# Two norms in front of first panels: raw scaled residual multiplied chunk by chunk, token factor applied at the evacuation

## The chip, the cores and the metric

One Trainium2 chip, one core. The metric is the device time of one execution in microseconds (us). The kernel before was timed three times: 2372.38 us median, 2368.09 lowest, 2375.34 highest. One more execution was profiled; all rows below come from it.

## The reference, cut to what matters

Two transformer stages run one after the other on 256 tokens of width 1024. The first has two layers with feed-forward blocks and attention; its result passes through a norm (`norm_final`) and goes straight into the second stage, which begins with a norm of its own (`norm_mix_2`) and a projection `w_in_2` into four groups of columns. At its end the second stage adds `merged @ w_o`, norms again (`norm_ffn_2`, no shift) and multiplies with `ffn_w_up_2`, then a short convolution over the tokens, a gated product and a last down projection.

What matters here is that each of the two norms is `x * r(token) * gain(feature)`, where `r` is the inverse root of the token's mean square, and that a matrix product follows it. The token factor stands outside the sum over features, so `(x * r * gain) @ W` equals `r * ((x * gain) @ W)`.

## The kernel before, in words

**Layout.** The residual `h` is held as 8 chunks of 128 features (partitions) by tokens; in the part that matters only the 256 tokens of the first stream. Weights come from DRAM as panels: one panel is 16 tiles of 128x128 in the phases here, 1 MB, and gives two output chunks. `st.load` (L500 to L510) issues a panel's DMA on SP into one of two `raw` buffers, once the buffer's last reader is done.

**Three products.** Every float32 product is made from split operands: `hi` is a rounded copy, `lo` the rest. `three` (L1181) issues three matmuls for one tile: whi with u_hi, whi with u_lo, wlo with u_hi. A panel of these phases is 8 chunks by 2 outputs by 3, or 48 matmuls of 128x256. Splitting a panel costs ACT one copy (L566) and DVE one subtraction (L568). `split` (L558 to L569) is issued one panel ahead.

**Order.** All engines run queues in program order. `Stream.run` (L626 to L715) writes it: for each group the split of the next panel, the evacuation of the last group, then the product of this one; PE waits for its panel's `s_lo` (L672) and for the evacuation two groups back (L674). With `split_first` the split stands ahead of the evacuation. Panel 1 of a phase that follows a norm is not split by `split` but in four quarters, `split_hi` and `split_lo` (L599 to L624), placed between the steps of the norm. The last of them, quarter 3 of `lo`, raises `s_lo` for panel 1, and it is issued at the very end of `norm` (L1172).

**The norm.** Squares of the chunks are added into `ssq` as the chunks of `h` are finished (`add_square`, L980); the last chunk's square is kept apart (`last_squares`, L999). `norm_scale` (L1026) has PE add over the features with one-column products (L1037, L1040), ACT takes the root (L1052), DVE the inverse (L1055) and spreads it on a diagonal (L1056), and PE turns that into a row factor in a PSUM bank (L1064). `norm` (L1081) then makes `u_hi` and `u_lo` of all chunks: the first two one by one (L1110, L1126, L1136), then three pairs (L1118, L1145, L1148, L1153). At both places of the change the first panel's product goes chunk by chunk behind this (L1196 to L1200, and L1992 to L1995), so that each pair of chunks is multiplied as soon as it is there.

**First norm** (after `down2` of layer 1, ahead of `rwkv_in`): called with `twice`, it makes the factor of two norms in a row, bank 5, and the factor of the first, bank 4. After it come a memset, a small DVE operation for `rest_mu` (L1958), the scaling of `h` in place (`scaled_rows`, L1887, in four pairs), and the side panels. `side_panels` (L2048) issues panel n in four quarters and, after the first quarter of panel n, the evacuation of panel n-1 (`side_evac`, L2005) and then the split of panel n+1. For `rwkv_in` the evacuation is two ACT copies for each output, L2014 and L2015, and one DVE operation, L2022. Panel 2's first three quarters are followed on PE by the `w_a_g` products (L2122), which wait for a sigmoid and a tanh on ACT (L2117, L2118), and everything of the second stage follows these. While this norm runs, POOL builds `rel_bias_map`.

**Second norm** (after `w_o`, ahead of `up_2`): one factor. `w_o` has four groups and `split_first`; its evacuation `wo_evac` (L2855) adds two chunks to `h` and squares them. `up_evac` (L2892) copies a group's two outputs to `conv_in` and makes `conv_out` from the same banks on ACT, then the taps on DVE.

These few lines set the order in the norm:

```
        for x in parts:
            pe.after(*(squared if x == 1 and twice else [squared[x]]))
            act.after(pe.do(sums(x, tmp, False, True)))
...
        marks = [None, None]
        for x in parts:
            pe.after(scaled[x])
            marks[x] = pe.do(pe.q.matmul(banks[4 + x][:, 0:S], cst("ones"), diag[:, x * S:(x + 1) * S], start=True, stop=True))
...
        before[0](*before[1:])
        if ph:
            st.split_lo(ph, 1, 3)
```

Of the kernel before, what the change touches and what calls it, by code (L numbers as in the profile page):

```python
# [16 lines left out]
F32 = mybir.dt.float32  # L17
# [5 lines left out]
P = 128  # L23
D = 1024
KC = D // P
S = 256
# [691 lines left out]
def build(nc, ins, out):  # L718
# [32 lines left out]

    sil = [sb(f"sil{i}", [P, T]) for i in range(2)]
# [273 lines left out]
    def norm_scale(n, twice=False, then=None):  # L1026

        parts = (1, 0) if twice else range(n // S)  # L1030
        tmp, squared = last_square

        def sums(x, src, start, stop):

            for t in range(2):
                both = twice and x == 1
                m = pe.q.matmul(banks[4 + x][:, t:t + 1], src[:, x * S + t * P:x * S + (t + 1) * P], cst("ones", 1),  # L1037
                                start=start and t == 0, stop=stop and t == 1 and not both)
                if both:
                    m = pe.q.matmul(banks[5][:, t:t + 1], src[:, t * P:(t + 1) * P], cst("eps", 1),  # L1040
                                    start=False, stop=stop and t == 1)
# [213 lines left out]
    def down(name, n, gates, hidden, then, weight=None):  # L1255

        q0 = sq_count[0]
# [11 lines left out]
        def evacuate(m, par, G, done):  # L1269
# [9 lines left out]
        def square(m, par, G):  # L1279
# [5 lines left out]
            add_square(at(m), n, count=k, weighted=weighted)  # L1285

# [86 lines left out]
    for l in range(L1):  # L1373
# [500 lines left out]
        if last:  # L1874
            both_gains = sb("both_gains", [P, KC])
            dve.do(dve.q.tensor_tensor(both_gains[:, :], vcol("norm_final", 0, KC), vcol("norm_mix_2", 0, KC), ALU.mult))
        down(("down2", l), streams * S, mod_gate(l, 2), hid, "rwkv_in" if last else ("up1", 1), "norm_final" if last else None)
# [16 lines left out]
    ready = norm(1, lambda c, s: (both_gains[:, c:c + 1], None), "rwkv_in", twice=True)  # L1894
# [52 lines left out]
    def place(name, shape, at_, dt=F32):  # L1947
# [17 lines left out]
                [("mla_in", k) for k in range(2)] + [("gate_in", k) for k in range(12)]  # L1965
    s_side = nc.alloc_semaphore("side_panel_evacuated")
# [10 lines left out]
    def side_target(n, b):  # L1977
        if n == 0:
            return banks[2 + b][:, 0:S]
        return banks[6 + n % 2][:, b * S:(b + 1) * S]  # L1980

    def side_quarter(n, q):
# [8 lines left out]
        if n == 0:  # L1991
            for kc in range(2 * q, 2 * q + 2):  # L1992
                pe.after(ready[kc])
                for b in range(2):
                    r = three(side_target(0, b), tile_of(slot, b * KC + kc), chunk_of(u_one, kc, 0, S), kc == 0, kc == KC - 1)  # L1995
        for kc in range(4 * (q % 2), 4 * (q % 2) + 4) if n else ():
# [3 lines left out]
            else:  # L2000
                r = three(side_target(n, b), tile_of(slot, b * KC + kc), chunk_of(u_one, kc, 0, S), kc == 0, kc == KC - 1)
# [3 lines left out]
    def side_evac(n):  # L2005
# [3 lines left out]
        if name == "rwkv_in":  # L2009
            for b in range(2):  # L2010
# [3 lines left out]
                copied = act.do(act.q.activation(buf[:, 1:S + 1], side_target(n, b), ACT.Copy))  # L2014
                r = act.q.activation(mix[:, c, :], side_target(n, b), ACT.Copy, scale=rest_mu[:, c:c + 1])  # L2015
# [839 lines left out]
    def wo_evac(m, par, G, done):  # L2855
# [28 lines left out]
    first.append(ready)  # L2884
# [7 lines left out]
    def up_evac(m, par, G, done):  # L2892
        act.q.wait_ge(st.s_pe, at(done))
        if not m.static() or m.base >= 2:
            act.q.wait_ge(s_tap, m.times(4).plus(-4))
            act.q.wait_ge(s_cp, m.plus(-1))
        for b in range(2):
            act.q.activation(cu[par][:, b, 2:S + 2], banks[2 * par + b][:, 0:S], ACT.Copy)  # L2898
        for b in range(2):
            r = act.q.activation(cv[par][:, b, :], banks[2 * par + b][:, 0:S], ACT.Identity,  # L2900
# [29 lines left out]
    st.run("up_2", pair_multiply, up_evac, second=up_product, third=up_hidden, early=True, ahead=True, split_first=True)  # L2930
# [54 lines left out]
```

## Time and profile before

| | us |
|---|---|
| median of three runs | 2372.38 |
| lowest, highest | 2368.09, 2375.34 |
| time of the profiled execution | 2373.76 |
| its span in the trace | 2372.4 |
| PE busy | 2264.7 (95%) |
| DVE busy | 1499.0 (63%) |
| ACT busy | 955.8 (40%) |
| POOL busy | 368.8 (16%) |

The profiled execution took 1.4 us more than its span, and 1.4 us more than the median of the three runs. Busy times are sums over one engine; PE's records overlap in a pipeline, so that a record of 0.28 us follows the one before by 0.12. In a row of the timeline the bracket is the idle time of that engine just before and what ended it.

### The profile page before, as it was taken

How to read it: one execution, taken by the hardware profiler on the slowest of the kernel's cores; microseconds unless marked ns; L12 is line 12 of the kernel's file. 1: busy time of each engine (PE TensorE's matmuls, PEld its weight loads, DVE VectorE, ACT ScalarE, POOL GpSimd, SP SyncE). 2: the span in 40 equal slices, each digit the busy share in tenths (PEclk: the TensorE clock that was granted, in tenths of full speed). 3: DMA queues.
4: the chain of work that ended last, by engine and by line, in shares of the span. 5: the costliest groups of instructions: out<-in, count | busy, mean ns of one | idle time of the engine just before them, and what ended most of it. 6: DMA issues, size and time to landing. Idle time of an engine off the chain costs nothing. (4 is left out here: it accounts for less than half of the span.)

```text
span 2372.4 us, 36948 instructions
## 1 busy us (share of the span) xinstructions
PE 2264.7 (95%) x14328; PEld 1921.8 (81%) x14328; DVE 1499.0 (63%) x2311; ACT 955.8 (40%) x1534; POOL 368.8 (16%) x365
## 2 busy tenths in 40 slices
PE   6999999999999999999999998989999999998998
PEld 4888887766678888878888876669998998898998
DVE  4666766555575666666565345556667766876874
ACT  4222223455442222242222244544446425555763
POOL 1000001000000000000000010039996476000000
PEclk9999999999999999999999999999999999999999
DMA  7554445101134444434443242124544232244544
GB/s 277 190 188 170 173 166 180 71 36 54 54 118 175 159 177 174 168 119 177 159 177 127 98 136 72 54 73 158 190 170 159 102 118 72 89 144 159 179 172 146
DMA packets 52614, 331.03 MB, mean 140 GB/s; under 512 B 6544, under 2 KB 7824, under 8 KB 21648
## 3 DMA queue, kind: packets, MB, share of 16 engines
q1 hardware_dynamic: 49040, 319.15, 37.4%
q0 software_dynamic: 3456, 10.25, 1.4%
q8 instruction: 82, 1.34, 0.2%
q14 instruction: 36, 0.29, 0.0%
HBM read 325.56 MB, written 3.80 MB: 139 GB/s over the span
## 5 line engine op out<-in xcount | busy, mean ns | idle before, releaser
L1183 PE MATMUL bank<-u_hi,whi 128*128 128x512 f32 (+1 forms) x2512 | 868.2, 346 | 36.4 <-DVE u_lo L1137 13.6
L1184 PE MATMUL bank<-u_lo,whi 128*128 128x512 f32 (+1 forms) x2512 | 851.6, 339 | 0.0
L1185 PE MATMUL bank<-u_hi,wlo 128*128 128x512 f32 (+1 forms) x2512 | 851.2, 339 | 0.0
L568 DVE TENSOR_TENSOR wlo<-raw,whi 128x2048 fp32r<-128x2048 f32 (+2 forms) x207 | 435.0, 2102 | 316.1 <-ACT whi L566 315.9
L1183 PEld LDWEIGHTS bank<-u_hi,whi 128*128 128x128 f32 x2512 | 478.8, 191 | 111.1 <-issue 29.0
L1185 PEld LDWEIGHTS bank<-u_hi,wlo 128*128 128x128 f32 x2512 | 478.9, 191 | 52.3
L1184 PEld LDWEIGHTS bank<-u_lo,whi 128*128 128x128 f32 x2512 | 479.6, 191 | 49.2 <-issue 0.2
L566 ACT ACTIVATE whi<-raw 128x2048 fp32r<-128x2048 f32 (+2 forms) x207 | 353.0, 1705 | 340.2 <-PE bank L1185 263.1
L1245 ACT ACTIVATE sil<-bank 128x512 f32<-128x512 f32 (+1 forms) x88 | 48.0, 545 | 544.7 <-PE bank L1185 544.7
L1183 PE MATMUL bank<-hidden_hi,whi 128*128 128x512 f32 x528 | 205.4, 389 | 0.0
L1184 PE MATMUL bank<-hidden_lo,whi 128*128 128x512 f32 x528 | 205.4, 389 | 0.0
L1185 PE MATMUL bank<-hidden_hi,wlo 128*128 128x512 f32 x528 | 205.4, 389 | 0.0
L1249 DVE TENSOR_TENSOR prod<-sil,bank 128x512 f32<-128x512 f32 (+1 forms) x88 | 54.6, 621 | 172.2 <-ACT sil L1245 168.5
L921 DVE SCALAR_TENSOR_TENSOR bank<-raw,c_row 128x1024 f32<-128x1024 f32 x128 | 157.2, 1228 | 2.1 <-DMA raw<-in_stream 2.0
L589 DVE TENSOR_TENSOR wlo<-raw,whi 128x1024 fp32r<-128x1024 f32 (+2 forms) x82 | 97.3, 1200 | 92.6 <-ACT whi L581 83.7
L921 DVE SCALAR_TENSOR_TENSOR raw<-raw,bank 128x1024 f32<-128x1024 f32 x128 | 155.8, 1217 | 0.0
L1363 POOL TENSOR_TENSOR rel_bias_map<-rel_bias_map,bucket_step 128x384 f32<-128x384 f32 x124 | 152.3, 1228 | 10.4
L1413 POOL DMA_DIRECT2D tables<-in_const x2 | 1.1, 575 | 965.6 <-PE bank L1185 965.6
L1360 POOL TENSOR_SCALAR bucket_step<-in_bucket,bucket_steps 128x384 f32<-128x384 f32 x124 | 132.8, 1071 | 12.4
L1184 PEld LDWEIGHTS bank<-hidden_lo,whi 128*128 128x128 f32 x528 | 99.1, 188 | 20.7
L1185 PEld LDWEIGHTS bank<-hidden_hi,wlo 128*128 128x128 f32 x528 | 99.1, 188 | 20.6
L1183 PEld LDWEIGHTS bank<-hidden_hi,whi 128*128 128x128 f32 x528 | 99.1, 188 | 20.4
(426 smaller groups left out, 2913.3 us busy)
## 6 DMA issues: line engine op xcount, KB each, us to landing
raw<-in_stream SPq DMA_DIRECT2D x231, 1024.0 KB, 4.8
raw<-in_stream SPq DMA_DIRECT2D x80, 704.0 KB, 4.0
first_ada<-in_stream SPq DMA_DIRECT2D x8, 1024.0 KB, 16.3
raw<-in_stream SPq DMA_DIRECT2D x8, 768.0 KB, 4.3
skew<-rpb_rows POOLq DMA_DIRECT2D x8, 336.0 KB, 6.4
nbr_bias<-skew POOLq DMA_DIRECT2D x24, 112.0 KB, 3.3
h<-in_tokens SPq DMA_DIRECT2D x1, 2048.0 KB, 11.6
uq_ukv<-in_small POOLq DMA_DIRECT2D x1, 1536.0 KB, 8.0
```

The costliest lines, as they stand in the source:

```text
L566: a.activation(self.hi[to][:, 0:n], raw[:, 0:n], ACT.Copy).then_inc(self.s_hi, 1)
L568: v.tensor_tensor(self.lo[to][:, 0:n], raw[:, 0:n], self.hi[to][:, 0:n].bitcast(F32), ALU.subtract).then_inc(self.s_lo, 1)
L589: r = v.q.tensor_tensor(self.lo[to][:, cols], self.raw[slot][:, cols], self.hi[to][:, cols].bitcast(F32), ALU.subtract)
L921: r = dve.q.scalar_tensor_tensor(out=product, in0=w, scalar=1.0, in1=rows, op0=ALU.mult, op1=ALU.mult, accum_out=to)
L1183: pe.q.matmul(dst, w[0], x[0], start=start, stop=False)
L1184: pe.q.matmul(dst, w[0], x[1], start=False, stop=False)
L1185: return pe.q.matmul(dst, w[1], x[0], start=False, stop=stop)
L1245: act.q.activation(sil[par][:, 0:n], banks[2 * par][:, 0:n], ACT.Silu).then_inc(s_sil, 1)
L1249: dve.q.tensor_tensor(prod[par][:, 0:n], sil[par][:, 0:n], banks[2 * par + 1][:, 0:n], ALU.mult).then_inc(st.s_ev, 1)
L1360: z = pool.do(pool.q.tensor_scalar(step[:, :], bucket[:, :], 1.0 - start, steps[:, hh, b + 1:b + 2], ALU.add, ALU.mult))
L1363: z = pool.do(pool.q.tensor_tensor(rel[:, hh, :], rel[:, hh, :], step[:, :], ALU.add))
L1413: pool.q.dma_start(tab[:, :], ins["const"][:, CC.kept:CC.at["causal"]]).then_inc(s_tab, 16)
```

## The change

`u_raw` is a new hi and lo pair of the residual times the norm's gain, without the token factor, in columns of `u_hi` and `u_lo` that are free then. `raw_chunk` makes one chunk of it, one ACT copy and one DVE operation, behind the square of that chunk. `first_on_raw` gives three pieces of the first panel's product on `u_raw`: `early`, chunks 0 to 2, ahead of the norm's sums; `late`, chunks 3 to 6, behind the sums and ahead of the product that makes the row factor; and the last chunk, behind it. For `rwkv_in` the first two panels use `u_raw`, for `up_2` the first. The factor is copied from its bank to SBUF behind the norm, and the outputs of these panels are multiplied by it on DVE at their evacuation; ACT then works from that result. Panel 1 of `up_2` takes the normed chunks one by one. The quarter split of panel 1 begins behind the raw chunk instead of ahead of the last square.

```diff
+    u_raw = [nc.alloc_sbuf_tensor_at(f"u_raw_{n}", [P, KC, T], F32R,
+                                     offset=H_AT + KC * T * 4 * (1 + i) + 4 * (S + APART))[:, :, 0:S]
+             for i, n in enumerate(("hi", "lo"))]
...
+    def raw_chunk(c, gain, k):
+
+        act.q.activation(u_raw[0][:, c, :], h[:, c, 0:S], ACT.Copy, scale=gain).then_inc(s_raw_hi, 1)
+        dve.q.wait_ge(s_raw_hi, k.plus(1))
+        dve.q.scalar_tensor_tensor(out=u_raw[1][:, c, :], in0=h[:, c, 0:S], scalar=gain,
+                                   in1=u_raw[0][:, c, :].bitcast(F32), op0=ALU.mult, op1=ALU.subtract).then_inc(s_raw_lo, 1)
+
+    def first_on_raw(then, dst, freed):
+
+        ph, r0 = PHASE[then], raw_count[0]
+        raw_count[0] += KC
+
+        def chunk(kc):
+            pe.q.wait_ge(s_raw_lo, r0 + kc + 1)
+            for b in range(2):
+                r = three(dst[b][:, 0:S], tile_of(ph.first % 2, b * KC + kc), chunk_of(u_raw, kc, 0, S), kc == 0, kc == KC - 1)
+            return r
+
+        def early():
+            pe.q.wait_ge(st.s_lo, ph.first + 1)
+            pe.q.wait_ge(st.s_ev, freed)
+            for kc in range(3):
+                chunk(kc)
+
+        def late():
+            for kc in range(3, KC - 1):
+                chunk(kc)
+
+        return early, late, lambda: chunk(KC - 1)
+
+    def copy_factor(mark, bank):
+
+        dve.after(mark)
+        return dve.do(dve.q.tensor_copy(factor, bank[:, 0:S]))
+
+    def norm_scale(n, twice=False, then=None, late=None):
...
             scaled[x] = r
+        if late:
+            late()
         marks = [None, None]
...
-                last_squares(n, marks, k, weighted, then)
+                last_squares(n, marks, k, weighted, None if raw_gains is not None else then)
+                if raw_gains is not None:
+                    raw_chunk(KC - 1, raw_gains[:, KC - 1:KC], Count(r0 + KC - 1))
+                    st.split_hi(PHASE[then], 1, 0)
...
             add_square(at(m), n, count=k, weighted=weighted)
+            if raw_gains is not None:
+                raw_chunk(at(m), raw_gains[:, bass.ds(m.plus(0), 1)], Count(r0 + m.base, m.step, m.reg))
...
-    ready = norm(1, lambda c, s: (both_gains[:, c:c + 1], None), "rwkv_in", twice=True)
+    raw_bank = 2 * (st.groups % 2)
+    early, late, side_first = first_on_raw("rwkv_in", banks[raw_bank:raw_bank + 2], st.groups - 1)
+    early()
+    rd = norm_scale(S, True, "rwkv_in", late)
+    ready = norm(1, lambda c, s: (both_gains[:, c:c + 1], None), "rwkv_in", twice=True, rd=rd)
+    factor_ready = copy_factor(rd[1], banks[5])
...
+        if n == 0 and q == 3:
+            r = side_first()
+        x = u_raw if n < RAW_PANELS else u_one
+        if n >= RAW_PANELS and q == 0 and n == RAW_PANELS:
+            pe.after(*ready)
...
-                copied = act.do(act.q.activation(buf[:, 1:S + 1], side_target(n, b), ACT.Copy))
-                r = act.q.activation(mix[:, c, :], side_target(n, b), ACT.Copy, scale=rest_mu[:, c:c + 1])
+                if n < RAW_PANELS:
+                    dve.q.wait_ge(st.s_pe, PHASE[name].first + k + 1)
+                    dve.after(factor_ready)
+                    copied = dve.do(dve.q.tensor_tensor(buf[:, 1:S + 1], side_target(n, b), factor, ALU.mult))
+                    act.after(copied)
+                else:
+                    copied = act.do(act.q.activation(buf[:, 1:S + 1], side_target(n, b), ACT.Copy))
+                r = act.q.activation(mix[:, c, :], buf[:, 1:S + 1] if n < RAW_PANELS else side_target(n, b), ACT.Copy,
+                                     scale=rest_mu[:, c:c + 1])
...
-            last_squares(S, [(st.s_ev, G.plus(1))], then="up_2")
+            last_squares(S, [(st.s_ev, G.plus(1))])
         else:
             act.q.wait_ge(st.s_ev, G.plus(1))
             add_square(2 * m.base + 1, S)
+        for c in (2 * m.base, 2 * m.base + 1):
+            raw_chunk(c, vcol("norm_ffn_2", c), Count(raw_count[0] + c))
+        if m.base == KC // 2 - 1:
+            st.split_hi(PHASE["up_2"], 1, 0)
...
-    ready = norm(1, lambda c, s: (vcol("norm_ffn_2", c), None), "up_2")
+    early()
+    rd = norm_scale(S, False, "up_2", late)
+    ready = norm(1, lambda c, s: (vcol("norm_ffn_2", c), None), "up_2", rd=rd)
+    factor_ready = copy_factor(rd[0], banks[4])
...
+        first_panel = m.static() and m.base == 0
+        if first_panel:
+            dve.q.wait_ge(st.s_pe, at(done))
+            dve.after(factor_ready)
         for b in range(2):
-            act.q.activation(cu[par][:, b, 2:S + 2], banks[2 * par + b][:, 0:S], ACT.Copy)
+            if first_panel:
+                act.after(dve.do(dve.q.tensor_tensor(cu[par][:, b, 2:S + 2], banks[2 * par + b][:, 0:S], factor, ALU.mult)))
+            else:
+                act.q.activation(cu[par][:, b, 2:S + 2], banks[2 * par + b][:, 0:S], ACT.Copy)
```

## Rows read from the trace of the kernel before

**Rows 1.** The page, busy time, share of the span and instructions of each engine.

```profile
PE 2264.7 (95%) x14328; PEld 1921.8 (81%) x14328; DVE 1499.0 (63%) x2311; ACT 955.8 (40%) x1534; POOL 368.8 (16%) x365
```

**Rows 2.** Windows: length, busy of PE, PEld, DVE, ACT, POOL, granted clock, DMA, GB/s.

```profile
1797.20:1814.50 17.30, 13.03 (x77) 10.83 (x76) 14.37 (x26) 8.74 (x19) 15.93 (x16) 0.80 0.35 120
2163.40:2180.10 16.70, 11.23 (x58) 10.01 (x59) 11.30 (x26) 10.50 (x22) 0.00 (x0) 0.69 0.18 63
2180.10:2185.70 5.60, 5.60 (x50) 5.60 (x49) 3.19 (x4) 3.37 (x5) 0.00 (x0) 1.00 0.52 187
```

**Rows 3.** Timeline, first norm, DVE: start, us, engine, line, operation.

```profile
1795.91 2.65 DVE L568 TENSOR_TENSOR wlo<-raw,whi 128x2048 fp32r<-128x2048 f32 x1 [2.18 <-ACT whi L566]
...
1803.30 0.87 DVE L1110 SCALAR_TENSOR_TENSOR sil<-h,both_gains,bank 128x256 f32<-128x256 f32 x2 [0.17 <-PE bank L1064]
...
1812.85 0.68 DVE L621 TENSOR_TENSOR wlo<-raw,whi 128x512 fp32r<-128x512 f32 x1
...
1814.13 0.89 DVE L1958 TENSOR_SCALAR one_less_mu<-vec 128x14 f32<-128x14 f32 x1
...
1815.16 1.66 DVE L1887 SCALAR_TENSOR_TENSOR h<-h,vec,bank 128x256 f32<-128x256 f32 x4
...
1818.45 2.79 DVE L568 TENSOR_TENSOR wlo<-raw,whi 128x2048 fp32r<-128x2048 f32 x1 [0.84 <-ACT whi L566]
```

**Rows 4.** Timeline, first norm, ACT.

```profile
1799.47 0.40 ACT L1012 ACTIVATE prod<-h 128x256 f32<-128x256 f32 x1
...
1815.50 0.47 ACT L2015 ACTIVATE mixed<-bank,one_less_mu 128x256 f32<-128x256 f32 x1
...
1816.48 1.94 ACT L566 ACTIVATE whi<-raw 128x2048 fp32r<-128x2048 f32 x1
...
1821.61 1.93 ACT L566 ACTIVATE whi<-raw 128x2048 fp32r<-128x2048 f32 x1
```

**Rows 5.** Timeline, first norm and panels behind it, PE.

```profile
1799.92 0.38 PE L1037 MATMUL bank<-const,prod 128*128 128x1 f32 x2 [1.49 <-ACT prod L1012]
...
1800.83 0.79 PE L1037 MATMUL bank<-const,prod 128*128 128x1 f32 x4
...
1802.04 2.36 PE L1064 MATMUL bank<-inv_norm_diagonal,const 128*128 128x256 f32 x4 [0.42 <-DVE inv_norm_diagonal L1056]
...
1825.73 1.34 PE L2122 MATMUL bank<-mixed,w_a_g 64*128 64x256 f32 x5
```

**Rows 6.** Short windows around changes of the granted clock, columns as in rows 2.

```profile
1801.00:1802.00 1.00, 0.63 (x4) 0.54 (x3) 0.84 (x4) 0.60 (x3) 0.92 (x2) 0.53 0.93 297
1807.00:1808.00 1.00, 0.99 (x5) 0.69 (x4) 0.82 (x2) 1.00 (x4) 0.92 (x2) 0.56 0.00 0
1842.00:1843.00 1.00, 1.00 (x7) 1.00 (x6) 0.19 (x1) 1.00 (x1) 0.00 (x0) 0.51 0.00 0
2174.00:2176.00 2.00, 2.00 (x10) 1.77 (x10) 1.91 (x4) 1.97 (x5) 0.00 (x0) 0.50 0.00 0
2176.00:2177.00 1.00, 1.00 (x8) 1.00 (x8) 1.00 (x2) 1.00 (x3) 0.00 (x0) 0.74 0.00 0
```

**Rows 7.** Timeline, PE: products of few columns ahead of the clock's fall at 1842.

```profile
1839.53 1.92 PE L2187 MATMUL bank<-const,v_tokens 128*128 128x2 f32 x16 [0.43 <-ACT v_tokens L2171]
```

**Rows 8.** Timeline, second norm, ACT, DVE and PE.

```profile
2158.93 1.90 ACT L566 ACTIVATE whi<-raw 128x2048 fp32r<-128x2048 f32 x1
...
2160.86 2.29 DVE L568 TENSOR_TENSOR wlo<-raw,whi 128x2048 fp32r<-128x2048 f32 x1 [1.37 <-ACT whi L566]
...
2166.23 0.99 PE L1037 MATMUL bank<-const,ssq 128*128 128x1 f32 x4 [2.84 <-DVE ssq L995]
...
2169.08 1.22 PE L1064 MATMUL bank<-inv_norm_diagonal,const 128*128 128x256 f32 x2 [1.01 <-DVE inv_norm_diagonal L1056]
...
2171.88 0.55 PE L1183 MATMUL bank<-u_hi,whi 128*128 128x256 f32 x1 [1.57 <-DVE u_lo L1136]
...
2178.54 0.69 DVE L621 TENSOR_TENSOR wlo<-raw,whi 128x512 fp32r<-128x512 f32 x1
```

More of the change, by code:

```diff
@@ L1024, in build @@
     split_u = {}
-    def norm_scale(n, twice=False, then=None):
+    s_raw_hi = nc.alloc_semaphore("raw_chunk_hi_done")
+    s_raw_lo = nc.alloc_semaphore("raw_chunk_lo_done")
+    raw_count = [0]
+    factor = diag[:, S:T]
+    def raw_chunk(c, gain, k):
[24 more added lines that the diff above has]
+    def norm_scale(n, twice=False, then=None, late=None):
         parts = (1, 0) if twice else range(n // S)
@@ L1253, in gate_up, with down @@
         hidden_count[0] += FC
-    def down(name, n, gates, hidden, then, weight=None):
-        q0 = sq_count[0]
+    def down(name, n, gates, hidden, then, weight=None, raw_gains=None):
+        q0, r0 = sq_count[0], raw_count[0]
         pe.after((s_hl, hidden_count[0] - 1))
@@ L1875, in build @@
             both_gains = sb("both_gains", [P, KC])
-            dve.do(dve.q.tensor_tensor(both_gains[:, :], vcol("norm_final", 0, KC), vcol("norm_mix_2", 0, KC), ALU.mult))
-        down(("down2", l), streams * S, mod_gate(l, 2), hid, "rwkv_in" if last else ("up1", 1), "norm_final" if last else None)
+            gains_done = dve.do(dve.q.tensor_tensor(both_gains[:, :], vcol("norm_final", 0, KC), vcol("norm_mix_2", 0, KC), ALU.mult))
+            dve.after(gains_done)
+            act.after(gains_done)
+        down(("down2", l), streams * S, mod_gate(l, 2), hid, "rwkv_in" if last else ("up1", 1), "norm_final" if last else None,
+             both_gains if last else None)
         if l == 0:
@@ L1965, in build @@
                 [("mla_in", k) for k in range(2)] + [("gate_in", k) for k in range(12)]
+    RAW_PANELS = 2
     s_side = nc.alloc_semaphore("side_panel_evacuated")
@@ L1978, in side_target @@
         if n == 0:
-            return banks[2 + b][:, 0:S]
+            return banks[raw_bank + b][:, 0:S]
         return banks[6 + n % 2][:, b * S:(b + 1) * S]
@@ L1990, in side_quarter @@
                 pe.q.wait_ge(s_side, n - 1)
[L1991 to L1995, printed above, removed]
+        if n == 0 and q == 3:
[3 more added lines that the diff above has]
+            pe.after(*ready)
         for kc in range(4 * (q % 2), 4 * (q % 2) + 4) if n else ():
@@ L2000, in side_quarter @@
             else:
-                r = three(side_target(n, b), tile_of(slot, b * KC + kc), chunk_of(u_one, kc, 0, S), kc == 0, kc == KC - 1)
+                r = three(side_target(n, b), tile_of(slot, b * KC + kc), chunk_of(x, kc, 0, S), kc == 0, kc == KC - 1)
         if q == 3:
@@ L2867, in wo_evac @@
             add_square(2 * m.base + 1, S)
+        for c in (2 * m.base, 2 * m.base + 1):
+            raw_chunk(c, vcol("norm_ffn_2", c), Count(raw_count[0] + c))
+        if m.base == KC // 2 - 1:
+            st.split_hi(PHASE["up_2"], 1, 0)
     st.run("w_o", pair_multiply, wo_evac, early=True, split_first=True)
-    ready = norm(1, lambda c, s: (vcol("norm_ffn_2", c), None), "up_2")
+    par = st.groups % 2
+    early, late, up_first = first_on_raw("up_2", banks[2 * par:2 * par + 2], st.groups - 1)
+    early()
+    rd = norm_scale(S, False, "up_2", late)
+    ready = norm(1, lambda c, s: (vcol("norm_ffn_2", c), None), "up_2", rd=rd)
+    factor_ready = copy_factor(rd[0], banks[4])
     over = [pe.last(), act.last(), (st.s_pe, st.panels_done("w_o"))]
@@ L2883, in build, with up_multiply @@
     h0 = hidden_count[0]
-    first.append(ready)
+    up_calls = [ready, None]
+    def up_multiply(par, part, slot):
+        if len(up_calls) == 2:
+            up_calls.pop()
+            return up_first()
+        return pair_products(par, slot, u_one, S, up_calls.pop() if up_calls else None)
     def vdyn(name, m, b):
@@ L2896, in up_evac @@
             act.q.wait_ge(s_cp, m.plus(-1))
+        first_panel = m.static() and m.base == 0
+        if first_panel:
+            dve.q.wait_ge(st.s_pe, at(done))
+            dve.after(factor_ready)
         for b in range(2):
-            act.q.activation(cu[par][:, b, 2:S + 2], banks[2 * par + b][:, 0:S], ACT.Copy)
+            if first_panel:
+                act.after(dve.do(dve.q.tensor_tensor(cu[par][:, b, 2:S + 2], banks[2 * par + b][:, 0:S], factor, ALU.mult)))
+            else:
+                act.q.activation(cu[par][:, b, 2:S + 2], banks[2 * par + b][:, 0:S], ACT.Copy)
         for b in range(2):
-            r = act.q.activation(cv[par][:, b, :], banks[2 * par + b][:, 0:S], ACT.Identity,
+            src = cu[par][:, b, 2:S + 2] if first_panel else banks[2 * par + b][:, 0:S]
+            r = act.q.activation(cv[par][:, b, :], src, ACT.Identity,
                                  scale=vdyn(("conv_w", 2), m, b), bias=vdyn("conv_b", m, b))
@@ L2929, in build @@
     root_table(ACT.Silu)
-    st.run("up_2", pair_multiply, up_evac, second=up_product, third=up_hidden, early=True, ahead=True, split_first=True)
+    st.run("up_2", up_multiply, up_evac, second=up_product, third=up_hidden, early=True, ahead=True, split_first=True)
     hidden_count[0] += FC
```

## The prediction

> **What bounds the kernel now.** I read the page first. PE is busy for 95% of the span [rows 1], so a saving must come from where PE is not multiplying panels, or multiplies at the lower clock. Then the windows of the two norms. From the last matmul in front of the first norm to the end of the first panel behind it 17.3 us pass, and 16.7 us at the second; the granted clock is 0.80 and 0.69 of full there [rows 2]. A panel of 48 matmuls alone takes 5.6 us at full clock [rows 2], 0.117 us a matmul; at half clock, 1.2 GHz, ten records fill 2.00 us, about 0.21 each [rows 6]. So 11.7 and 11.1 us at the two places are not panel work at full speed, and that is what the change reaches for.
>
> Next I asked what PE waits for, in the timelines. The norm's row factor reaches DVE at 1803.30, and the work on ACT and DVE behind it ends with the last quarter of panel 1's weights, at 1812.85 + 0.68 = 1813.53 [rows 3]. Panel 0 is multiplied in between, a pair of chunks at a time, and ends at about 1814.4, the end of the first window [rows 2]. At the second norm the factor is there at 2169.08 + 1.22 = 2170.30, the last quarter at 2179.23 [rows 8], panel 0 ends at 2180.1 [rows 2]. This decides the case: **the chain on ACT and DVE, not panel 0, fills the time**, and panel 0 sticks out by only 0.9 us at each place. PE can't begin panel 1 before that last quarter, and the change leaves the quarter where it is, at the end of the norm.
>
> **The change, part by part.** Raw chunks: eight ACT copies and eight DVE operations at each norm, 0.40 to 0.47 us and about 0.41 each (ACT by L1012 and L2015 of the same size, DVE by four L1887 in 1.66) [rows 3, 4]. In the down projection they stand beside PE's panels, and PE's timeline has no wait there; cost 0, and if the cover is too short, at most their own 8 x 0.41, 3.3 us. Evacuating on DVE, adding the factor copy and the ordering are not covered, as follows.
>
> **First norm.** Panel 0's split ends at 1795.91 + 2.65 = 1798.56 [rows 3]. PE can begin `early` there, 18 x 0.117 = 2.1 us, to 1800.7. The sums over `ssq`, now done in PE's wait for that split and the last square, come behind. The like sums over the last square, 12 records, take from 1799.92 to 1801.62, 1.7 us [rows 5]; so both are done at 1800.7 + 3.4 = 1804.1 instead of 1801.62, 2.5 later. Then `late`, 24 matmuls, in front of L1064: 2.8 us at full clock, 5.0 at half. 0.4 of it replaces the wait for the diagonal [rows 5]. Last L1064: 1.26 us from its start to DVE's at half clock [rows 3, 5], about 0.6 less at full. The factor is late by 2.5 + 2.4 - 0.6 = 4.3 us at full clock and 2.5 + 4.6 = 7.1 at half.
>
> Which clock? Before, it fell at 1801 to 1802, after some 2.5 us of few-column sums and waits [rows 5, 6]. At 1842 it is half though PE looks busy: what PE did just before was 16 products of two columns, 1.9 us, behind a wait of 0.43 [rows 6, 7]. [...] I let it fall during `late` and take **+6**. Before, half clock in these places cost nothing, as PE waited for chunks anyway; now it delays everybody.
>
> The chain itself is unchanged: last quarter at 1813.5 + 6 = 1819.5. PE, done with panel 0 by about 1811, idles for some 8 us, and panel 1 starts at half clock; before, it came back at about 2176.5 [rows 6], 4.6 us after panel 0's first product at 2171.88 [rows 8], and at the first norm at 1807.9 [rows 6], some 3 us after it (1.6 from factor to first product, as at the second). That stretch costs half of itself, 1.5 to 2.3 us. It does not matter here, because panel 2 is later still. Behind the last quarter DVE has the factor copy, 0.4 (as an L1887), then L1958 and four L1887, which end at 1816.8 + 6.4 = 1823.2 [rows 3]. Only then comes the evacuation of panel 0, which was ACT's alone: now DVE multiply, ACT scale, DVE mix, and the same again, in turn. Until ACT is free that is 0.41 + 0.47 + 0.41 + 0.41 + 0.47 [rows 3, 4] and some hand-overs, 2.4 us. ACT's split of panel 2 starts at 1825.6, not 1816.48 [rows 4]; DVE's part follows 1.97 later and should take 2.29 as at [rows 8] instead of 2.79, POOL being done by then. Panel 2's weights are ready at 1829.9, not 1821.2: +8.6. Before, the evacuation of panel 1 and the split of panel 3 ran on ACT while PE multiplied panel 2, from 1821.61 [rows 4]. Now DVE does four more L1887, 1.6, and the alternating evacuation, 2.4, ahead of it: 1833.9, **+12.3**. The `w_a_g` products follow that split after the sigmoid and the tanh, 4.1 us later, at 1825.73 before [rows 5], and the whole second stage follows them. First norm: +12, from +10.4 (clock held until the factor) to +15 (half clock throughout, and again for the `w_a_g` products after PE's idle time).
>
> **Second norm.** ACT's split of `up_2`'s panel 0 starts when ACT is free, at 2158.93 [rows 8]; two raw copies more in front: +0.65, and DVE's split and the residual behind it likewise. The raw operations of chunks 4 and 5 delay the last residual and squares by 0.8: the sums start at 2167.7 instead of 2166.23 [rows 8]. They and L1064 should be at full clock now, since `early` fills the wait of 2.84: 0.7 and 0.6 less than before. `late` adds 2.8 less the wait of 1.0 it replaces. Factor: +1.5 - 0.7 + 1.8 - 0.6 = **+2.0**, and the last quarter is at 2181.2. Panel 1 starts then instead of 2180.1, +1.1, and at half clock after 8 us without work: +1.9, between the 1.5 and 2.3 above. The evacuation of panel 0, now DVE's first, ends before panel 1 does. Second norm: **+3**, from +1.1 (clock held) to +6 (half clock in `late` and L1064 too).
>
> Sum: 12 + 3 = 15. The profiled execution of 2373.8 (span 2372.4 and 1.4 around it) becomes 2388.8; it lies 1.4 over the median, so the median becomes 2387.4, rounded to 2387. Bounds of this case: +11 to +21, 2384 to 2394.
>
> **A rule against this.** The Trainium skill, "TensorE: Matmul & The Clock Gate", under "HAM oscillation", says that idle gaps of PE are what brings its clock down, and that work should be arranged so that PE stays warm. By it filling the gap before the factor is right, and the clock would be held up to L1064. That gives the third rival, whose terms come from the rows alone.
>
> **Rivals.** (1) Faster: PE's panel work is the bound after all, and panel 0 under the norm saves its 5.6 us at both places: -11, 2361. It decides if the last quarter of panel 1 lands earlier by as much, so that panel 1 starts as panel 0 ends. Against it stand the 10.2 us from factor to last quarter, of a window in which DVE is busy for 14.4 of 17.3 us [rows 2], and that its start is later, not earlier. Chance 0.06. (2) No difference: the alternating evacuations hide behind panels 1 and 2, so that at the first norm only the factor's 4.3 at full clock counts, and at the second 1.1: +5, 2378. For it: DVE waited 0.84 for ACT before [rows 3]. Against: `scaled_rows` stands ahead of the evacuation. Chance 0.14. (3) The clock is held through the sums: +10.4 and +1.1, 2384, still slower. Chance 0.2. (4) My forecast, 0.6.
>
> **How the numbers follow.** A measurement of this kernel can tell about 0.3%, 7.1 us, from no change. Faster is rival 1, 0.06; the same is rival 2, 0.14; slower the rest, 0.80. The range takes in cases 3 and 4 and the upper part of 2: 2376 to 2394.
>
> **What would show it.** In the changed trace L1064's successor on DVE starts 9 to 12 us behind panel 0's split, not the 4.7 of now; panel 0 ends well before panel 1's last quarter; PE waits there some 8 us for DVE's split; panel 1 starts at half clock; ACT waits for DVE's factor products between the two outputs. I am wrong if panel 1 begins within 1 us of panel 0's end, or if DVE's chain from factor to last quarter is much under 10 and 9 us.

## The result and the profile after

The kernel got slower: 2393.79 us median of four runs (2390.91 to 2396.65), against 2370.89 (2368.09 to 2375.34) in four runs of the kernel before beside them. The ratio is 1.0091, with a 95% interval of 1.0076 to 1.0107, so 21.6 us, 18.0 to 25.4. All differences between kernels below are such ratios turned into us; the two medians here lie 22.9 us apart. The forecast was 2387, its range ended at 2394, and "slower" had 0.80.

The page of the profiled execution of the changed kernel (2393.94 us, span 2392.4), answering to [rows 1]:

```profile
PE 2269.1 (95%) x14328; PEld 1926.9 (81%) x14328; DVE 1511.3 (63%) x2335; ACT 961.2 (40%) x1544; POOL 367.1 (15%) x365
```

PE multiplies as often as before, x14328, and is busy 4.4 us longer. So the other 15.6 of the 20.0 us that the span gained are idle time of PE.

Timeline of PE after, first norm and the panels behind it, answering to [rows 5]:

```profile
1801.56 0.36 PE L1229 MATMUL bank<-u_raw_hi,whi 128*128 128x256 f32 x1 [0.87 <-issue]
...
1805.90 0.58 PE L1081 MATMUL bank<-const,prod 128*128 128x1 f32 x4
1806.35 0.36 PE L1229 MATMUL bank<-u_raw_hi,whi 128*128 128x256 f32 x1
...
1810.77 1.03 PE L1110 MATMUL bank<-inv_norm_diagonal,const 128*128 128x256 f32 x4
...
1821.41 0.58 PE L1229 MATMUL bank<-u_raw_hi,whi 128*128 128x256 f32 x1 [8.91 <-DVE wlo L621]
...
1838.76 1.34 PE L2189 MATMUL bank<-mixed,w_a_g 64*128 64x256 f32 x5 [3.29 <-ACT mixed L2185]
```

`early` and the sums run from 1801.56 to 1806.35, `late` from there to 1810.77, the factor's product behind it. Panel 0 ends at about 1812.5, and then PE waits 8.91 us for the last quarter of panel 1's weights. Before, PE went from panel 0 into panel 1 without a wait. The work was moved ahead, and a wait opened behind it.

Windows after, columns as in [rows 2]:

```profile
1806.00:1807.00 1.00, 1.00 (x9) 1.00 (x9) 0.53 (x2) 0.73 (x3) 0.90 (x2) 0.80 0.92 383
1807.00:1808.00 1.00, 1.00 (x7) 1.00 (x7) 0.80 (x3) 0.31 (x1) 0.92 (x2) 0.50 0.95 399
1810.00:1811.00 1.00, 1.00 (x10) 0.97 (x10) 0.00 (x0) 0.00 (x0) 0.91 (x2) 0.99 0.00 0
1812.00:1821.00 9.00, 0.50 (x5) 0.29 (x3) 8.21 (x12) 6.27 (x13) 7.05 (x7) 0.77 0.00 0
1821.00:1824.00 3.00, 2.58 (x12) 2.59 (x13) 2.70 (x12) 0.00 (x0) 0.00 (x0) 0.50 0.41 117
1842.00:1846.00 4.00, 4.00 (x18) 3.50 (x17) 3.17 (x18) 2.47 (x7) 0.00 (x0) 0.50 0.31 129
...
2187.00:2188.00 1.00, 1.00 (x11) 1.00 (x10) 0.00 (x0) 0.00 (x0) 0.00 (x0) 1.00 0.00 0
```

The granted clock falls to half inside `late`, is back (0.99) when the factor's product starts, is half again as panel 1 starts, and a third time behind the wait for `w_a_g`. At the second norm it is at full up to the factor. While PE is busy for 0.50 of 9 us, DVE is busy for 8.21: this points to DVE as the bound, and experiment 4 tests it.

Timelines of DVE and ACT after, first norm, answering to [rows 3, 4]:

```profile
1803.19 0.69 DVE L1039 SCALAR_TENSOR_TENSOR u_raw_lo<-h,both_gains,u_raw_hi 128x256 fp32r<-128x256 f32 x1 [1.35 <-ACT u_raw_hi L1037]
1803.80 1.48 DVE L621 TENSOR_TENSOR wlo<-raw,whi 128x512 fp32r<-128x512 f32 x1
...
1811.40 0.88 DVE L1156 SCALAR_TENSOR_TENSOR sil<-h,both_gains,bank 128x256 f32<-128x256 f32 x2 [3.57 <-PE bank L1110]
...
1820.68 0.68 DVE L621 TENSOR_TENSOR wlo<-raw,whi 128x512 fp32r<-128x512 f32 x1
...
1822.69 1.66 DVE L1941 SCALAR_TENSOR_TENSOR h<-h,vec,bank 128x256 f32<-128x256 f32 x4 [0.21 <-DVE one_less_mu L2017]
1824.26 0.42 DVE L2077 TENSOR_TENSOR shifted<-bank,inv_norm_diagonal 128x256 f32<-128x256 f32 x1
1825.40 0.48 DVE L2089 SCALAR_TENSOR_TENSOR mixed<-shifted,vec,mixed 128x256 f32<-128x256 f32 x1 [0.73 <-ACT mixed L2081]
1825.81 0.42 DVE L2077 TENSOR_TENSOR shifted<-bank,inv_norm_diagonal 128x256 f32<-128x256 f32 x1
1826.87 0.48 DVE L2089 SCALAR_TENSOR_TENSOR mixed<-shifted,vec,mixed 128x256 f32<-128x256 f32 x1 [0.64 <-ACT mixed L2081]
1828.61 2.29 DVE L568 TENSOR_TENSOR wlo<-raw,whi 128x2048 fp32r<-128x2048 f32 x1 [1.25 <-ACT whi L566]
```

```profile
1824.79 0.51 ACT L2081 ACTIVATE mixed<-shifted,one_less_mu 128x256 f32<-128x256 f32 x1 [5.04 <-DVE shifted L2077]
1826.26 0.51 ACT L2081 ACTIVATE mixed<-shifted,one_less_mu 128x256 f32<-128x256 f32 x1 [0.96 <-DVE shifted L2077]
1826.67 1.90 ACT L566 ACTIVATE whi<-raw 128x2048 fp32r<-128x2048 f32 x1
...
1834.37 0.51 ACT L2081 ACTIVATE mixed<-shifted,one_less_mu 128x256 f32<-128x256 f32 x1 [0.96 <-DVE shifted L2077]
1834.78 1.90 ACT L566 ACTIVATE whi<-raw 128x2048 fp32r<-128x2048 f32 x1
```

DVE waits 3.57 us for the factor. The last quarter ends at 1821.36, and ACT, idle for 5.04 us, gets the first output of panel 0 only behind `scaled_rows`; then the two engines take turns, each waiting for the other. ACT's split of panel 2 starts at 1826.67 (1816.48 in [rows 4]), that of panel 3 at 1834.78 (1821.61).

Second norm after, PE, answering to [rows 8]:

```profile
2184.24 0.60 PE L1081 MATMUL bank<-const,ssq 128*128 128x1 f32 x4 [0.74 <-DVE ssq L999]
...
2188.06 0.59 PE L1110 MATMUL bank<-inv_norm_diagonal,const 128*128 128x256 f32 x2
...
2197.62 0.58 PE L1229 MATMUL bank<-u_hi,whi 128*128 128x256 f32 x1 [8.26 <-DVE wlo L621]
```

The same picture: the factor's product stands behind 24 matmuls, and the last quarter comes 8.26 us after panel 0 is done.

**Where the 20 us of the span came from.** Two executions also drift apart where the code is the same. ACT's split of `down2`'s first panel stands ahead of everything that the change adds, and in the changed kernel's profile it is 3.15 us later than in before's. ACT before, then ACT after:

```profile
1728.59 1.37 ACT L566 ACTIVATE whi<-raw 128x1408 fp32r<-128x1408 f32 x1
```

```profile
1731.74 1.37 ACT L566 ACTIVATE whi<-raw 128x1408 fp32r<-128x1408 f32 x1
...
1742.78 1.38 ACT L566 ACTIVATE whi<-raw 128x1408 fp32r<-128x1408 f32 x1 [1.48 <-DVE both_gains L1927]
```

At the last residual of `down2` it is 2.9 us late. So I read each event's lateness against before, and its growth from one event to the next; "beyond the drift" below means less the lateness of that last residual in the same profile:

| event | late in us | growth |
|---|---|---|
| last residual of `down2` | 2.9 | drift |
| first product with the factor (1811.40 - 1803.30) | 8.1 | 5.2 |
| last quarter of panel 1 ends (1821.36 - 1813.53) | 7.8 | -0.3 |
| split of panel 2 on ACT | 10.2 | 2.4 |
| split of panel 3 on ACT | 13.2 | 3.0 |
| evacuation of the `w_a_g` products to `g` | 16.0 | 2.8 |
| first residual of `w_o` | 16.0 | 0 |
| split of `up_2`'s panels 3 and 4 | 19.7 | 3.7 |

From the last residual on the first norm costs 13.1, the second 3.7, and 2.9 was there already.

### The profile page after: what moved, and what is told of

Read it like the earlier page. It is cut to its first block and busy times, and to the rows that moved or that the text cites. A ratio compares the mean times of both kernels' runs of the same rounds, so it can differ in the third digit from the quotient of the medians.

```text
span 2392.4 us, 36997 instructions
## 1 busy us (share of the span) xinstructions
PE 2269.1 (95%) x14328; PEld 1926.9 (81%) x14328; DVE 1511.3 (63%) x2335; ACT 961.2 (40%) x1544; POOL 367.1 (15%) x365
## 5 line engine op out<-in xcount | busy, mean ns | idle before, releaser
L1229 PE MATMUL bank<-u_hi,whi 128*128 128x512 f32 (+1 forms) x2464 | 855.4, 347 | 41.0 <-DVE u_lo L1183 13.6
L1230 PE MATMUL bank<-u_lo,whi 128*128 128x512 f32 (+1 forms) x2464 | 839.8, 341 | 0.0
L1231 PE MATMUL bank<-u_hi,wlo 128*128 128x512 f32 (+1 forms) x2464 | 839.0, 341 | 0.0
L1229 PEld LDWEIGHTS bank<-u_hi,whi 128*128 128x128 f32 x2464 | 471.1, 191 | 114.1 <-issue 26.2
L1231 PEld LDWEIGHTS bank<-u_hi,wlo 128*128 128x128 f32 x2464 | 470.7, 191 | 51.8
L1230 PEld LDWEIGHTS bank<-u_lo,whi 128*128 128x128 f32 x2464 | 471.3, 191 | 49.9 <-issue 0.2
L1414 POOL TENSOR_TENSOR rel_bias_map<-rel_bias_map,bucket_step 128x384 f32<-128x384 f32 x124 | 158.8, 1281 | 10.4
L1411 POOL TENSOR_SCALAR bucket_step<-in_bucket,bucket_steps 128x384 f32<-128x384 f32 x124 | 126.6, 1021 | 12.4
```

The source lines that it names most:

```text
L1229: pe.q.matmul(dst, w[0], x[0], start=start, stop=False)
L1230: pe.q.matmul(dst, w[0], x[1], start=False, stop=False)
L1231: return pe.q.matmul(dst, w[1], x[0], start=False, stop=stop)
L1411: z = pool.do(pool.q.tensor_scalar(step[:, :], bucket[:, :], 1.0 - start, steps[:, hh, b + 1:b + 2], ALU.add, ALU.mult))
L1414: z = pool.do(pool.q.tensor_tensor(rel[:, hh, :], rel[:, hh, :], step[:, :], ALU.add))
```

## The experiments

Ten kernels, each timed beside the kernel before: five runs each, but four of `e7` and eleven or twelve of `e2`, `e6` and `e8`. Ratios are to that kernel; diffs are to the changed kernel, `...` marks what is cut from them.

**1. Each norm alone.** `e1_first_norm_only` restores the second norm, `e2_second_norm_only` the first.

```diff
-    rd = norm_scale(S, False, "up_2", late)
-    ready = norm(1, lambda c, s: (vcol("norm_ffn_2", c), None), "up_2", rd=rd)
...
+    ready = norm(1, lambda c, s: (vcol("norm_ffn_2", c), None), "up_2")
```

```diff
...
-    RAW_PANELS = 2
+    RAW_PANELS = 0
...
```

> The change at the first norm alone; the second norm as before. My theory (the chain from the factor to the next panels is late, and the evacuations on DVE add to it): the first norm costs some 13 of the change's 20 us in the profiles, so +13 to +17 us over before. In its trace DVE's first use of the factor comes 9 to 10 us behind the end of panel 0's split, and the w_a_g products 27 us behind the last residual add of down2, as in the changed kernel. Rival (the raw chunks themselves and the wait for the gains cost, in the two projections): the down projection is where the time goes, and the stretch from the last residual add to the w_a_g products is not over 17 + 5 us.

> The change at the second norm alone. My theory: +3 to +4 us over before, as the distance from the w_o phase's first panel to up_2's third panel grew by 3.7 us in the profiles; the two parts add up to the whole. Rival (the clock or DMA state carried from the first norm into the rest of the second stage makes up part of the 20): this alone gives 0 to 1, and the first norm alone the whole 20.

`e1`: 2388.88 us, ratio 1.006 (1.0047 to 1.0073), 14.2 us; its profile repeats the changed kernel's at the first norm within 0.1 (the factor 5.2 late beyond the drift, the splits 7.3 and 10.3, `g` 13.1). `e2`: 2379.66, ratio 1.0028 (1.0019 to 1.0037), 6.6 us. But `e2` kept a line of the change that made PE wait for all normed chunks ahead of panel 0 of `rwkv_in`:

```profile
1812.03 0.55 PE L1229 MATMUL bank<-u_hi,whi 128*128 128x256 f32 x1 [4.46 <-DVE u_lo L1199]
```

Its split of panel 2 was 4.2 us late beyond its drift, a cost of its own, so it doesn't measure the second norm. `e8_second_norm_clean` is `e2` without that line:

```diff
-        if n >= RAW_PANELS and q == 0 and n == RAW_PANELS:
+        if False:
             pe.after(*ready)
```

> As e2_second_norm_only, but without a wait of that kernel's own: there PE waited for all normed chunks in front of the first rwkv_in panel, which the kernel before does not. My theory: the stretch up to panel 2 of rwkv_in is as before, and the second norm alone costs 3 to 4 us. Rival: the second norm costs nothing by itself, and e2's time was that wait.

2375.93, ratio 1.0017 (1.0007 to 1.0027), 4.0 us, and 3.7 in its profile. So the rival that the second norm costs nothing by itself fell. Together 14.2 + 4.0 = 18.2, within the interval of the whole change, at its lower end.

**2. `late` behind the factor's product.** `e3_late_behind_factor` moves two lines.

```diff
-        if late:
-            late()
         marks = [None, None]
         for x in parts:
             pe.after(scaled[x])
...
+        if late:
+            late()
```

> The changed kernel with chunks 3 to 6 of the first panel (24 matmuls) issued behind the product that makes the row factor, at both norms. My theory: PE's order is what delays the factor, so it comes about 3.6 to 4.4 us earlier at the first norm and 1.8 to 2 at the second, everything behind it with it, and the time falls by 5 to 7 us against the changed kernel: some +13 to +17 over before. Panel 1 still waits for the last quarter of its weights. Rival (panel 0 on PE sets the end): the same 24 matmuls are only moved, and the time stays within 2 us of the changed kernel.

2387.78, ratio 1.0062 (1.0049 to 1.0075), some 7 us less than the change. DVE of this kernel:

```profile
1805.93 0.43 DVE L1100 TENSOR_TENSOR inv_norm_diagonal<-const,inv_norm 128x256 f32<-128x256 f32 x1
...
1807.67 0.87 DVE L1156 SCALAR_TENSOR_TENSOR sil<-h,both_gains,bank 128x256 f32<-128x256 f32 x2 [0.18 <-PE bank L1108]
```

DVE waits 0.18 us for the factor instead of 3.57. The factor is late by 2.2 beyond the drift instead of 5.2, the sums behind `early`, and the second norm costs 1.8 instead of 3.7. The order of 24 matmuls against one small product is worth 3.0 + 1.9 us in the profile.

**3. ACT evacuates as before.** `e4_act_evacuates` leaves the token factor of the raw panels out, and its copy: a part of the computation is missing, so as to have the old evacuation.

```diff
-    factor_ready = copy_factor(rd[1], banks[5])
...
-                if n < RAW_PANELS:
+                if False:
```

> The changed kernel with the panels on the raw residual evacuated by ACT straight from the bank as before; the token factor of these panels and its copy are left out. My theory: the alternating evacuation costs 5 us at the first norm (between the factor's +5 and the +10 at ACT's split of panel 3) and nothing at the second, since the panel 1 there is still being multiplied; -5 to -7 against the changed kernel, +13 to +17 over before. Rival (it hides behind panels 1 and 2): within 2 us of the changed kernel.

2384.01, ratio 1.004 (1.0027 to 1.0053), 12 us less than the change and more than I expected. Its ACT:

```profile
1819.99 0.39 ACT L2079 ACTIVATE shifted<-bank 128x256 f32<-128x256 f32 x1 [3.55 <-DVE one_less_mu L2016]
...
1820.89 0.49 ACT L2080 ACTIVATE mixed<-bank,one_less_mu 128x256 f32<-128x256 f32 x1
1821.24 1.93 ACT L566 ACTIVATE whi<-raw 128x2048 fp32r<-128x2048 f32 x1
```

Beyond the drift of 1.9 the split of panel 2 is 2.9 us late, not 7.3, and that of panel 3 5.3, not 10.3. Of the 5.0 us by which panel 3's split is earlier, 1.5 is the clock, which stayed at full in `late` (the factor is late by 3.7, not 5.2), and 3.5 the evacuation. Behind the `w_a_g` products the clock stayed at full too, and the 2.8 us are not lost there. That makes 7.8 of the 12 us; the second norm costs 3.6 here against 3.7, and where the other 4 us of the runs come from, the two profiles don't show. Windows of `e4`:

```profile
1806.00:1808.00 2.00, 2.00 (x20) 2.00 (x19) 1.15 (x3) 0.27 (x1) 1.82 (x3) 1.00 0.16 66
...
1842.00:1846.00 4.00, 4.00 (x36) 3.98 (x34) 3.97 (x10) 3.94 (x5) 0.00 (x0) 1.00 0.36 111
```

**4. Is panel 1's gate the bound, or what stands behind it?** The gate is the wait for the last quarter of its weights. `e5_quarters_ahead` takes the quarters of panel 1 out of the norm and does them on both engines while PE makes the factor, with `late` behind it as in `e3`.

```diff
+            for i in range(1, 4):
+                st.split_hi(PHASE[then], 1, i)
+            for i in range(1, 4):
+                st.split_lo(PHASE[then], 1, i)
...
-        if ph:
+        if ph and not rd_given:
             st.split_lo(ph, 1, 3)
```

> As e3_late_behind_factor, and quarters 1 to 3 of panel 1's weights are split directly behind the diagonal, ahead of the norm's own work on ACT and DVE. My theory (ACT and DVE are the bound at the first norm, PE's start of panel 1 at the second): at the first norm panel 1 starts right behind panel 0 instead of 8 us later, and yet ACT's split of panel 2 moves by less than 1.5 us, since DVE's work in front of it is the same; at the second norm panel 1 goes along with the chunks and the third panel comes 2 to 4 us earlier. Total 2 to 5 us less than e3: +10 to +13 over before. Rival (only the wait for the last quarter binds, at both norms): the whole 8 us of waiting goes at each, and the time falls to or below that of before.

2382.96, ratio 1.0053 (1.0039 to 1.0066). The last quarter is there 12.6 us before the change's (10.3 beyond the drift), and PE multiplies panel 1 right behind panel 0. Then:

```profile
1826.22 0.58 PE L1235 MATMUL bank<-u_hi,whi 128*128 128x256 f32 x1 [9.50 <-DVE wlo L568]
```

The wait of 8.91 became one of 9.50 a panel later. Net of drift the split of panel 2 is 5.0 us late, and `e3`, with the gate where it was, has 4.8. So panel 1's gate is where PE waits, but the sum of the work on DVE and ACT sets the end of the first norm: this is the run that settles the bound there. At the second norm I had expected a gain, and there was none: the split of panel 4 is 3.2 us late, against 1.8 in `e3`. PE no longer waits for the last quarter, but for the evacuation of panel 0, whose factor products on DVE stand behind the next split:

```profile
2191.88 0.58 PE L1235 MATMUL bank<-u_hi,whi 128*128 128x256 f32 x1 [4.75 <-ACT conv_out L2996]
```

**5. The second norm, mended.** `e6_second_reordered` keeps the first norm as before, and at the second has the quarters ahead, `late` behind the factor, the last chunks' raw `lo` parts in DVE's waits, and the two products with the factor ahead of the next split.

```diff
+    def raws_lo(cs):
+        for c in cs:
+            dve.q.wait_ge(s_raw_hi, raw_base + c + 1)
...
-    rd = norm_scale(S, False, "up_2", late)
+    rd = norm_scale(S, False, "up_2", late, lambda i: raws_lo(range(4 + 2 * i, 6 + 2 * i)))
```

> First norm as before. At the second: four raw chunks are multiplied ahead of the sums, the raw work of the last four chunks stands behind the squares, the factor product ahead of the rest of panel 0, the quarters of panel 1 directly behind the diagonal, the factor products of panel 0 on DVE ahead of the split of panel 2, and the table load for Silu behind panel 0's evacuation. My theory: with DVE's order mended the idea pays where DVE has slack; up_2's third panel starts 2 to 4 us earlier than before, -2 to -4 us in all, which is at the edge of what 5 rounds can tell. Rival (the raw work costs as much as it frees): within 1 us of before or slower.

2371.41, ratio 0.9999 (0.999 to 1.0008). Its PE:

```profile
2169.54 0.70 PE L1112 MATMUL bank<-inv_norm_diagonal,const 128*128 128x256 f32 x2 [1.31 <-DVE inv_norm_diagonal L1102]
...
2173.53 0.36 PE L1239 MATMUL bank<-u_hi,whi 128*128 128x256 f32 x1 [0.46 <-DVE u_lo L1192]
...
2176.37 0.39 PE L1239 MATMUL bank<-u_hi,whi 128*128 128x256 f32 x1 [1.03 <-DVE u_lo L1209]
```

The wait of 8.26 us is gone; the longest that is left in this stretch is 2.22 us, for the next panel's split on DVE. The profile is 1.8 us ahead over this stage (0.7 early at `w_o`'s first residual, 2.5 early at the split of panel 4), but the runs can't tell the kernel from the one before; the 2 to 4 us that I expected are not shown.

**6. Is the half clock a cost?** `e7_fill_second` puts 60 products that nobody reads into PE's wait at the second norm, `e9_fill_before_wag` 26 of them into the wait ahead of the `w_a_g` products.

```diff
+            pe.after((st.s_ev, st.groups))
+            for i in range(60):
+                pe.q.matmul(banks[2 * (1 - par)][:, 0:S], u_raw[1][:, i % KC, 0:P], u_raw[0][:, i % KC, :], start=True, stop=True)
```

```diff
+    pe.after((s_side, 1))
+    for i in range(26):
+        pe.q.matmul(banks[raw_bank][:, 0:S], u_raw[1][:, i % KC, 0:P], u_raw[0][:, i % KC, :], start=True, stop=True)
     pe.after(m0, mixed[12], wag_ready, (s_side, 1), x2[-1])
```

> The changed kernel with 60 matmuls of 128x256 whose result nobody reads (7.0 us at full clock) in PE's wait between up_2's panel 0 and panel 1. My theory: the half clock at the start of panel 1 costs about 1.9 us there; the granted clock stays at full, panel 1 ends that much earlier and the third panel's evacuation with it: -1 to -2 us against the changed kernel in the profile, too little for the medians. Rival (the evacuation of panel 0 through DVE binds, not panel 1's length): the clock is full and the distance from panel 1's start to the third split stays what it was, 19.7 behind before's.

> The changed kernel with 26 matmuls of 128x256 whose result nobody reads (3.0 us) in PE's wait of 3.3 us ahead of the w_a_g products. My theory: that wait is why the clock is at half from 1841 to 1847 in the changed kernel, and it costs the 2.9 us by which the copy of g is later than the decay (16.0 against 13.0 behind before); with the wait filled the two are equally late, and the profile is 2 to 3 us shorter, the median up to as much. Rival (the loss there is the order of ACT or DVE and not the clock): the 2.9 us stay.

`e7`: 2391.22, runs from 2384.17 to 2395.61, ratio 1.0092 (1.0076 to 1.0107), the same as the change. In its profile the clock is at full from 2189 to 2203, and the second norm costs 2.2 instead of 3.7, but the runs don't show it: inconclusive by time. `e9`: 2386.92, ratio 1.0066 (1.0053 to 1.008), 6 us less. Its windows, over `late` and from the first `w_a_g` product to `g`:

```profile
1807.68:1810.59 2.91, 2.91 (x27) 2.91 (x27) 1.71 (x4) 0.83 (x3) 2.64 (x4) 1.00 0.47 191
...
1839.34:1847.27 7.93, 7.93 (x53) 7.16 (x54) 4.18 (x21) 5.90 (x13) 0.00 (x0) 1.00 0.40 134
```

The same stretches of the changed kernel:

```profile
1806.35:1810.77 4.42, 4.42 (x27) 4.42 (x27) 1.33 (x4) 0.84 (x3) 3.96 (x6) 0.61 0.39 165
...
1838.76:1849.62 10.86, 10.86 (x50) 9.63 (x51) 5.32 (x22) 6.33 (x14) 0.00 (x0) 0.69 0.28 97
```

PE is busy for the whole of the second stretch in both, with the same products, so the lower clock costs 2.9 us there. But the profile of `e7`, whose first norm is the change's, loses nothing there either:

```profile
1827.66 0.39 PE L1229 MATMUL bank<-u_hi,whi 128*128 128x256 f32 x1 [2.26 <-DVE wlo L568]
...
1835.47 1.34 PE L2189 MATMUL bank<-mixed,w_a_g 64*128 64x256 f32 x5 [1.77 <-ACT mixed L2185]
```

In that execution PE waited 1.77 us, not 3.29, and kept its clock. All profiles with the change at the first norm fit this: with PE's wait ahead at 3.29 to 3.30 us (the change, `e1`, `e3`) the stretch ran at 0.69 and took 10.9 us, with 0.20 to 2.24 us (`e4`, `e5`, `e7`, `e9`, `e10`) at 1.00 and took 7.9. `e9` has the 26 products, some 3.0 us, in place of a wait. So the clock there goes with the wait, the loss falls on the executions with the long one, and the filler takes it away; no run shows what else might do it. Part of `e9`'s gain is of another place: `late` ran at full clock in its profile, 3.6 us of delay and not 5.2, ahead of any filler.

**7. All of it at the first norm.** `e10_first_mended` (second norm as before) has the sums that need only `ssq` ahead of `early`, two chunks in `early`, `late` behind the factor, and both products with the factor ahead of ACT's two scalings.

```diff
-    early()
-    rd = norm_scale(S, True, "rwkv_in", late)
...
+    rd = norm_scale(S, True, "rwkv_in", late, early)
...
+                both = [dve.do(dve.q.tensor_tensor(shift[(2 * k + b) % 4][:, 1:S + 1], side_target(n, b), factor, ALU.mult))
+                        for b in range(2)]
```

> The change at the first norm alone, with its order mended: the sums over the added squares in front of the early chunks (in PE's wait for panel 0's split, where they were), two early chunks instead of three, the rest of panel 0 behind the row factor, and at the evacuation both factor products on DVE first. My theory (e1's 14 us are the order, not the idea): the factor is within 1 us of before's, ACT's split of panel 2 1 to 3 us behind before's and that of panel 3 2 to 5; +2 to +5 us over before. Rival (raw work and DVE evacuation cost by themselves): +8 or more.

2379.89, ratio 1.0037 (1.0023 to 1.0051), 8.8 us, against the 14.2 of `e1`. Its profile is 4.2 late at `g`, of which 0.6 was there before. ACT:

```profile
1818.09 0.91 ACT L2085 ACTIVATE mixed<-shifted,one_less_mu 128x256 f32<-128x256 f32 x2 [5.65 <-DVE shifted L2074]
1818.90 1.90 ACT L566 ACTIVATE whi<-raw 128x2048 fp32r<-128x2048 f32 x1
...
1825.13 0.91 ACT L2085 ACTIVATE mixed<-shifted,one_less_mu 128x256 f32<-128x256 f32 x2 [4.32 <-DVE shifted L2074]
```

The factor is on time (0.6 late, as the last residual), the turns are gone, and the splits of panels 2 and 3 are still 1.8 and 3.7 us late beyond the drift. That is the evacuation's work on DVE itself: ACT's split of panel 2 starts 1.3 us behind the end of `scaled_rows`, where before it started 0.3 ahead of it. The profiled run is the fastest of its five, and its span is 4.3 us over before's, where the ratio says 8.8. By the profile my theory held (+2 to +5), by the runs its rival did (+8 or more), that the raw work and DVE's evacuation cost by themselves; this stays open. No version here beats the kernel before.

## Why the prediction held

**The bound.** "The chain on ACT and DVE, not panel 0, fills the time": right, and settled by `e5`. PE was to wait "some 8 us" for the last quarter; it waited 8.91 and 8.26. Rival 1, faster, fell with it.

**The number.** The median lies 0.2 us under the end of the range, and that is luck. I rounded the upper bound up: 2372.4 + 21 is 2393.4, and 2393.79 lies over it. Taken beside before's own four runs, at 2370.89, the change costs 21.6 us by the ratio and 22.9 by the medians, more than the 21 of my worst case.

**The factor at the first norm, +6.** Measured 5.2 beyond the drift in the change and in `e1`. The sums do end later, 2.0 us beyond the drift against the 2.5 forecast, and the clock fell inside `late`, as taken: 0.80 and then 0.50 in the windows. It was back by 1810, so the stretch lay between the two prices that I gave. At full clock I had 4.3; `e4` and `e9`, whose `late` ran at full clock, have 3.7 and 3.6. So rival 3's condition, a clock held through the sums, does occur in some executions of this code, and its price was 0.6 to 0.7 too high.

**The alternating evacuation, +9.1 and +12.3 at ACT's splits of panels 2 and 3.** 7.3 and 10.3 beyond the drift. The steps are the forecast ones, with ACT's waits of 0.96 between the outputs. Both terms were about 2 us too high: 0.8 by the factor, 0.3 by the stretch from factor to last quarter, and 0.7 by L1958, 0.89 us in [rows 3], which came later this time, with POOL done, and took 0.17 (L2017). The turns themselves, from the end of `scaled_rows` at 1824.35 to ACT's split, took 2.3 against the 2.4 forecast. Rival 2, evacuations that hide, fell with this: the two splits are 2.1 and 5.1 us later than the factor is.

**The second norm, +3.** Factor +2.3 (forecast +2.0), with the clock held through sums and `late`, as taken; 2.0 of it is there at the last residual of `w_o`, from the raw work in front of it, where I had 1.5. The stage cost 3.7 in the change and in `e8`'s profile, and 4.0 by `e8`'s runs. Panel 1 started at half clock, as forecast.

**The sum.** 15 forecast, 16.8 in the profile beyond the drift, 21.6 by the runs. The step that failed is the one that ends the first norm's sum: I put the half clock "again for the `w_a_g` products after PE's idle time" into the upper bound alone. In the profiled execution it happened, behind a wait of 3.29 us, and cost 2.8. With the two evacuation terms 2 too high, the first norm came out at 13.1 against 12: two errors that nearly cancel, so its closeness is luck too. The runs have 21.6 - 16.8 = 4.8 us more than the two norms in the profile, and `e1` and `e8` together, at 18.2, only 1.4 more. Each profile is one execution: before's lay 2.9 over the median of the four runs, which makes a difference of spans to it smaller. About 1 of the 4.8 is likely the raw work in `down2`, below. Which stretches run at half clock differs between executions too, and only one of each kernel was traced. So the rest of the 4.8 us is not explained by cause; that stays open.

**What I missed.** I put the raw chunks in `down2` at nothing, as PE had no wait there. The gains for both norms are now waited for by ACT: its split in front of `down2` stands 1.48 us behind them, and PE then waits 1.21 us for DVE's part of it. That was in the diff and should have had its sentence. In this profile `down2` absorbs it: 3.15 late at its start, 4.0 at its first residual, 2.9 at its last. But from the gains to the last residual the eight profiled kernels with raw chunks in `down2` take 0.3 us less to 1.2 us more than before, and the three without them (`e2`, `e6`, `e8`) 0.7 to 0.3 less. By the middle of each group, 0.6 more and 0.4 less, the raw work there costs about 1 us, which is my estimate and which "beyond the drift" hides.

## What to carry to other kernels

Filling an engine's wait with work moved ahead gains nothing, the clock aside, if that wait ends by another engine's chain: find who releases the engine after the filled stretch, and sum that chain with all that the change adds to it. In an in-order queue put the small product that others wait for ahead of the bulk, and don't let an evacuation go back and forth between two engines when one of them also splits the next panel. A second wait opened downstream can also bring the clock down there, so price each new wait twice, at both clocks.

## What the runs showed of the hardware

The clock's fall doesn't belong to a place in the code. The same 24 matmuls behind the same sums took 4.42 us at a granted clock of 0.61 in the changed kernel and 2.91 at 1.00 in `e9`, and the four runs of `e7` spread over 11 us.

Some DVE records are longer beside POOL's work: L621 took 1.48 us at 1803.80 and 0.68 at 1820.68, when POOL had ended, and `u_raw_lo` took 0.69 to 0.81 us each in `down2`, but 0.87 for two at the second norm, where POOL is idle. The 0.41 that I had taken for it was the unstretched price. Not every overlap does it: in [rows 3] L621 took 0.68 at 1812.85, in the middle of a record of POOL:

```profile
1812.47 1.42 POOL L1360 TENSOR_SCALAR bucket_step<-in_bucket,bucket_steps 128x384 f32<-128x384 f32 x1
```

That POOL is the cause was not tested by a run of its own.
